# Hybrid mixer and expert trunk on one core: the router fed from raw rows, gain and shift of the norm applied after the first gather

## Chip, cores and metric

One Trainium2 chip, 1 core. The metric is the device time of one execution in microseconds (us), as the median of several runs. PE is TensorE, DVE VectorE, ACT ScalarE, POOL GpSimd, SP SyncE.

## The reference, cut to what matters

Two layers over 256 tokens of width 1024. Each adds a mixer and then a channel mixer to alpha times x, with a layer norm after each. The channel mixer of layer 0 is a dense SwiGLU, that of layer 1 picks two of eight experts for each token.

```python
for l in range(DEPTH):
    mix = hybrid_mixer(x, ...)
    x = layer_norm(DEEPNORM_ALPHA * x + mix, ln1_g[l], ln1_b[l])
    ffn = swiglu(x, ...) if l % 2 == 0 else moe_swiglu(x, router_w[j], router_b[j], ...)
    x = layer_norm(DEEPNORM_ALPHA * x + ffn, ln2_g[l], ln2_b[l])

def layer_norm(x, g, b):
    mu, var = mean(x), mean((x - mean(x)) ** 2)
    return (x - mu) * rsqrt(var + LN_EPS) * g + b

# in moe_swiglu, for each token
logits = xt @ router_w + router_b
top_logit, top_idx = lax.top_k(logits, 2)
top_w = softmax(top_logit)
# each expert: (silu(xb @ wg) * (xb @ wu)) @ wd, weighted and added to the token's row
```

## The kernel before, in words

**Data.** Tokens lie in two tiles t of 128 rows; a row of 1024 is cut into 8 blocks k of 128, or two halves of 512. Weights stream through the core in pieces of 128x2048 (1 MB), 33 for the dense part and for each expert: A and B hold gate and up weights, D the down weights (FFORDER). SP's queue loads them into 17 slots, each as soon as its last user is through. To keep float32 accuracy, ACT copies each half of a piece rounded into whi (high part, ring of 3 pieces) and DVE subtracts to get low. A product is then three matmuls: high by high, high by low, low by high (L639 to L641; L832, L835, L838 for down pieces). This "split" is one ACT and one DVE operation of 128x1024 for each half piece. Activations are split in the same way.

**Expert jobs.** Eight jobs of one expert each, classes W and N in turn. A wide job (W, 128 token slots) splits its weights, a narrow one (N, 64 slots) uses them raw, with matmuls of L981 and L990. Job 0 is wide and always expert 7, so that its weights can be loaded before the router is done. In a wide job each engine runs through the 33 pieces i (L1030 on PE, L1400 on ACT, L1880 on DVE). At step i ACT and DVE split piece i + 2. After pieces B of chunk c, ACT makes silu (L1408), DVE the product he (L1883), PE transposes it (L853), ACT and DVE split the transpose (L1403, L1887), and a D piece uses it. Each engine works strictly in the order written; DVE's he of chunk c stands at step i = 3c + 1 (c over 0), ahead of the splits of that step. In job 0, steps 5 and 8 of ACT also make xh, steps 6 and 9 of DVE xl (L1850), the split rows of x for later gathers; step 22 of DVE makes S for the next job (L1843, L1845), for which it waits for POOL's places (tab_rdy, L1899); after piece 25 PE gathers rows for the next job.

**The second mixer's end and the router.** PE adds the last products of the mixer to PSUM tile by tile (down, L817). DVE's norm (L1544) takes mean and variance from PSUM (L1552, L1556), ACT the root (L1189), DVE the normed rows with gain and shift into x (L1562, L1566). PE transposes x (L623), ACT and DVE copy it to xT (L1197, L1534), PE multiplies by the router's weights (L1103). DVE adds the bias, finds the two largest of eight (L1803 to L1809), makes the one-hot mask mk (L1817). PE counts ranks with a triangular matrix (L1119 to L1121), DVE makes the selection matrix S (L1843), PE gathers and transposes the rows of job 0 in one step, x by S (L939), ACT and DVE split them to xgh and xgl (L1363, L1855), and job 0 begins. All steps take both tiles together. Between them PE runs filler products that nobody reads (keep_warm, L633; their numbers in WARM). DVE then makes the weights and hands counts over to POOL (tables, L1824 to L1834); POOL makes the order of jobs, the places of the tokens and their weights in some 70 small operations (job_tables, L491 to L579). ACT puts alpha times x into acc (L1355) during the router.

## Time and profile before

| what | value |
|---|---|
| median of 3 runs | 1027.97 us (1027.78 to 1028.08) |
| the profiled execution | 1027.9 us, its span 1026.1 us |
| mean granted TensorE clock | 0.996 |
| weights moved | 318 pieces of 1 MB, 334 GB/s over the span |
| last product of the second mixer to first product of job 0 | 352.03 to 366.73 us |
| job 0 on PE | 366.73 to 464.4 us |

The span is from the first to the last instruction; the 1.8 us around it belong to the execution. In the timeline a row merges equal operations; its second number is the time from the first one's start to the last one's end. Matmuls overlap, so the pitch from start to start is shorter than the duration shown.

### The profile page before, as it was taken

To read this page: it belongs to the slowest core of one execution; us is meant where nothing else is said; L and a number is where in the kernel's file an instruction comes from. 1 tells how busy PE (TensorE), PEld (TensorE's weight loads), DVE (VectorE), ACT (ScalarE), POOL (GpSimd) and SP (SyncE) were. 2 spreads that over 40 slices of the span, in tenths; PEclk is the share of its full clock that TensorE was granted. 3 is DMA by queue.
4 is the path that set the end of the run, shared out by engine and by line. 5 is a ranking of instruction groups with operands and counts; after the bars stand their busy time and mean duration, and the time that the engine had idled before them with its cause. 6 is when DMAs were issued, how large, how long until landed. Compare 5 with 4: busy or idle time off the path is not lost.

```text
span 1026.1 us, 15030 instructions
## 1 busy us (share of the span) xinstructions
PE 1005.4 (98%) x5878; PEld 765.8 (75%) x5878; DVE 644.9 (63%) x885; ACT 538.7 (52%) x822; POOL 86.0 (8%) x92
## 2 busy tenths in 40 slices
PE   9999999999999999999999999999999999999995
PEld 7977888888798887886567886558887556888552
DVE  6998554545679889981049993119986117997103
ACT  5786343444459677771147772128775116776112
POOL 0002000000200069910000000000000000000000
PEclk9999999999999999999999999999999999999998
DMA  9945454545584659989999999999999999999993
GB/s 370 383 160 210 174 193 177 201 172 201 219 335 148 232 190 352 370 335 395 421 420 421 421 421 421 419 422 421 420 422 422 419 422 421 419 422 421 420 420 149
DMA packets 48153, 343.23 MB, mean 335 GB/s; under 512 B 5376, under 2 KB 5504, under 8 KB 6864
## 3 DMA queue, kind: packets, MB, share of 16 engines
q1 hardware_dynamic: 46800, 337.14, 82.0%
q0 software_dynamic: 848, 4.51, 1.2%
q8 instruction: 48, 0.79, 0.3%
q10 hardware_dynamic: 432, 0.59, 0.2%
q14 instruction: 25, 0.20, 0.1%
HBM read 341.17 MB, written 1.05 MB: 334 GB/s over the span
## 4 chain that ended last, share of the span: by engine, by line
PE 88%; DVE 7%; ACT 3%; issue 1%; POOL 0%; POOLq 0%; DVEq 0%
PE bank L990 15%; PE bank L639 13%; PE bank L641 13%; PE bank L640 13%; PE bank L981 7%; PE bank L832 7%; PE bank L835 6%; PE bank L838 6%; DVE low L1868 2%; PE bank L853 1%; DVE low L1515 1%; PE bank L1072 1%; PE bank L633 1%; PE bank L623 1%; ACT scr L1281 1%
## 5 line engine op out<-in xcount | busy, mean ns | idle before, releaser
L1868 DVE TENSOR_TENSOR low<-raw,whi 128x1024 fp32r<-128x1024 f32 x246 | 290.6, 1235 | 21.6 <-ACT whi L1385 21.3
L1385 ACT ACTIVATE whi<-raw 128x1024 fp32r<-128x1024 f32 x246 | 242.2, 1051 | 0.3 <-PE bank L641 0.3
L990 PE MATMUL bank<-raw,xg 128*64 128x256 f32 x1312 | 150.1, 380 | 0.0
L1515 DVE TENSOR_TENSOR low<-raw,whi 128x1024 fp32r<-128x1024 f32 x110 | 131.3, 1223 | 25.6 <-ACT whi L1169 24.6
L639 PE MATMUL bank<-whi,xgh 128*128 128x512 f32 x352 | 141.7, 402 | 0.0
L1922 DVE TENSOR_TENSOR he<-he,bank 128x128 f32<-128x128 f32 x44 | 12.7, 289 | 202.5 <-ACT he L1445 202.5
L641 PE MATMUL bank<-whi,xgl 128*128 128x512 f32 x352 | 137.7, 391 | 0.0
L640 PE MATMUL bank<-low,xgh 128*128 128x512 f32 x332 | 129.3, 390 | 0.0
L1169 ACT ACTIVATE whi<-raw 128x1024 fp32r<-128x1024 f32 x114 | 115.8, 1058 | 25.2 <-PE bank L641 17.4
L990 PEld LDWEIGHTS bank<-raw,xg 128*64 128x64 f32 x1312 | 92.1, 137 | 43.2 <-issue 2.4
L639 PE MATMUL bank<-whi,ah 128*128 128x512 f32 (+1 forms) x240 | 92.2, 384 | 3.3 <-DVE al L1527 1.9
L641 PE MATMUL bank<-whi,al 128*128 128x512 f32 (+1 forms) x240 | 90.2, 376 | 0.0
L640 PE MATMUL bank<-low,ah 128*128 128x512 f32 (+1 forms) x240 | 90.0, 375 | 0.0
L981 PE MATMUL bank<-raw,hT 128*64 128x512 f32 x336 | 79.6, 594 | 0.0
L1445 ACT ACTIVATE he<-bank 128x128 f32<-128x128 f32 x44 | 12.2, 278 | 125.0 <-PE bank L990 125.0
L639 PEld LDWEIGHTS bank<-whi,xgh 128*128 128x128 f32 x352 | 66.1, 188 | 15.2 <-DVE low L1868 2.7
L641 PEld LDWEIGHTS bank<-whi,xgl 128*128 128x128 f32 x352 | 66.0, 188 | 14.7
L640 PEld LDWEIGHTS bank<-low,xgh 128*128 128x128 f32 x332 | 62.5, 188 | 11.9
L832 PE MATMUL bank<-whi,hth 128*128 128x512 f32 x224 | 70.2, 394 | 0.3 <-DVE htl L1887 0.3
L838 PE MATMUL bank<-whi,htl 128*128 128x512 f32 x224 | 69.1, 390 | 0.0
L835 PE MATMUL bank<-low,hth 128*128 128x512 f32 x216 | 66.7, 390 | 0.0
L639 PEld LDWEIGHTS bank<-whi,ah 128*128 128x128 f32 x240 | 45.2, 188 | 12.2 <-DVE al L1527 2.4
(310 smaller groups left out, 1376.5 us busy)
## 6 DMA issues: line engine op xcount, KB each, us to landing
raw<-W SPq DMA_DIRECT2D x303, 1024.0 KB, 16.7
spare<-W SPq DMA_DIRECT2D x15, 1024.0 KB, 17.8
scr<-gb_d POOLq DMA_DIRECT2D x3, 1024.0 KB, 5.0
x<-x_d SPq DMA_DIRECT2D x2, 512.0 KB, 5.6
raw<-W SPq DMA_DIRECT2D x2, 512.0 KB, 6.0
scr<-wbd_d POOLq DMA_DIRECT2D x2, 512.0 KB, 9.3
spare<-gb_d SPq DMA_DIRECT2D x1, 1024.0 KB, 14.5
out_d<-acc ACTq DMA_DIRECT2D x2, 256.0 KB, 2.5
```

The costliest lines, as they stand in the source:

```text
L639: nc.tensor.matmul(out, sh, mh, start=first, stop=False, skip_group_check=True)
L640: nc.tensor.matmul(out, sh, ml, start=False, stop=False, skip_group_check=True)
L641: return nc.tensor.matmul(out, sl, mh, start=False, stop=last, skip_group_check=True)
L832: nc.tensor.matmul(bank[:, 2 + 2 * t + n, :], sh, wh[:, n * 512:(n + 1) * 512], start=st, stop=False, skip_group_check=True)
L835: nc.tensor.matmul(bank[:, 2 + 2 * t + n, :], sh, wl[:, n * 512:(n + 1) * 512], start=False, stop=False, skip_group_check=True)
L838: last = nc.tensor.matmul(bank[:, 2 + 2 * t + n, :], sl, wh[:, n * 512:(n + 1) * 512], start=False, stop=en, skip_group_check=True)
L981: last = nc.tensor.matmul(bank[n * NARROW:(n + 1) * NARROW, 2, :], hT[:, c % 2, h * NARROW:(h + 1) * NARROW], w[:, h * D + n * 512:h * D + ...
L990: last = nc.tensor.matmul(bank[n * NARROW:(n + 1) * NARROW, c % 2, 0:FC].rearrange("p (a n) -> p a n", a=2), xg[:, kk, at:at + NARROW], gu ...
L1169: nc.scalar.activation(whi[:, p % SPLIT, h * HW:(h + 1) * HW], piece_slot(place(p)[0])[:, h * HW:(h + 1) * HW], ACT.Copy).then_inc(hi_rdy, 1)
L1385: nc.scalar.activation(whi[:, q % SPLIT, h * HW:(h + 1) * HW], piece_slot(home(J, i)[0])[:, h * HW:(h + 1) * HW], ACT.Copy).then_inc(hi_rd ...
L1515: V.tensor_tensor(low_of(p)[:, h * HW:(h + 1) * HW], piece_slot(place(p)[0])[:, h * HW:(h + 1) * HW], whi[:, p % SPLIT, h * HW:(h + 1) * H ...
L1868: V.tensor_tensor(low_slot(s)[:, h * HW:(h + 1) * HW], piece_slot(s)[:, h * HW:(h + 1) * HW], whi[:, q % SPLIT, h * HW:(h + 1) * HW].bitca ...
```

## The change

- **Router from raw rows.** ACT copies the mixer's raw sums y from PSUM into x, half a tile at a time (copy_y). PE transposes these, between the last products of the mixer (down_last), which are reordered so that half a tile is complete early. DVE multiplies the router's weights by the norm's gain and shift (gs, two operations of 128x64), PE adds their columns up, and DVE puts the norm into the logits: root's reciprocal times product, plus an offset from the mean and the column sums.
- **Rows.** ACT turns the raw rows into centred, scaled ones without gain and shift (centre, four operations of 128x512). The gather of job 0 reads these. Gain and shift, now along partitions, are applied after it: for the first half by DVE in four operations of 128x128, for the second by ACT in four (rows_first). The norm's four products of DVE and its copy to xT are gone. x itself gets gain and shift from DVE in four operations of 128x1024 in job 0, steps 3, 6, 9 and 12 (gain_shift); xh moves to ACT's steps 7 and 13, acc to its steps 16 and 19, xl to DVE's steps 17 and 20.
- **Tiles apart.** Choice, rank, S and gather are done for tile 0 and then for tile 1 (picks, places, gather_first). Small operations that took both tiles are now issued twice.
- **Job 0's start.** The splits of its first three pieces are done before it; its first two pieces are multiplied high parts first (first_products). DVE's tables come after all that; the counts of PE after the first piece. POOL no longer waits for x_rdy ahead of its tables, but still for DVE's.
- **Filler.** Of the router's 19 filler products one is left.
- rtab grows by gain and shift (16 columns); yh moves in SBUF, so that gb stays whole until job 0 has used it.

The diff, cut:

```diff
-XH_AT = {5: 0, 8: 1}
+GAIN_AT = {3: (0, 0), 6: (0, 1), 9: (1, 0), 12: (1, 1)}
+XH_AT = {7: 0, 13: 1}
+ACC0_AT = {16: 0, 19: 1}
...
-WARM = {"start": 8, "x1": 5, "mixer": 0, "dense": 0, "last_mixer": 0, "tile": 4, "tile2": 2, "split": 3, "rank": 7,
-        "slots": 3}
+WARM = {"start": 8, "x1": 5, "mixer": 0, "dense": 0, "slots": 1}
...
+            def down_last(p, act_t, t, ph):
+                order = [(0, 0), (0, 1), (1, 0), (1, 1)] if t or ph == 1 else [(0, 0), (1, 0), (0, 1), (1, 1)]
+                for n, k in order:
...
+                    if t == NT - 1 and ph == 1 and (n, k) in ((0, 1), (1, 0)):
+                        transpose_x(ph + 1, 0, (n,))
+                    elif t == NT - 1 and (n, k) == (0, 1):
+                        logits(0, (0,))
+                        column_sums()
+                    elif t == NT - 1 and (n, k) == (1, 0):
+                        transpose_x(ph + 1, 1, (0,))
...
+            def first_products(i, slot, wlow):
+                for k in range(4):
+                    if k % 2 == 0:
+                        pe.wait_ge(lo_rdy, 2 * (STREAM + i) + k // 2 + 1)
+                    if i == 0:
+                        pe.wait_ge(xg0_rdy, k + 1)
+                    elif k == 0:
+                        pe.wait_ge(xgh_rdy, 1)
...
+                pe.wait_ge(xgl_rdy, i + 1)
...
+            def gather_first(t, b, ks=range(4)):
+                pe.wait_ge(z_rdy, 2 * t + b + 1)
...
+                logits(0, (1,))
+                transpose_x(2 * DEPTH - 1, 1, (1,))
+                logits(1, (0, 1))
+                nc.tensor.matmul(bank[:, 1, 0:NE], ones, mk[:, 0, :], start=True, stop=False, skip_group_check=True)
+                pe.wait_ge(S0_rdy, 1)
+                gather_first(0, 0)
                 pe.wait_ge(mk_rdy, 1)
...
+                gather_first(0, 1)
+                keep_warm(WARM["slots"], 6)
+                pe.wait_ge(S_rdy, 1)
+                gather_first(1, 0)
+                gather_first(1, 1)
...
+                copy_y(0, 0)
+                copy_y(0, 1)
+                hi_half(p, 0)
+                root(0)
+                copy_xT(0, 0)
+                copy_xT(0, 1)
+                hi_half(p, 1)
+                copy_y(1, 0)
+                centre(0, 0)
+                copy_xT(1, 0)
+                copy_y(1, 1)
+                centre(0, 1)
+                root(1)
+                copy_xT(1, 1)
+                centre(1, 0)
+                centre(1, 1)
...
+            def rows_first():
+                for k in range(4):
+                    act.wait_ge(xv0_rdy, k + 1)
+                    nc.scalar.activation(xgh[:, k], first_rows[:, k], ACT.Copy).then_inc(xg0_rdy, 1)
+                act.wait_ge(xg0_ps, 2)
+                for k in range(4):
+                    turned_row(first_rows, 1, k).then_inc(xv_rdy, 1)
+                act.wait_ge(xv_rdy, 4)
+                nc.scalar.activation(xgh[:, 4:KT], first_rows[:, 4:KT], ACT.Copy).then_inc(xgh_rdy, 1)
...
+                    sums(0)
+                    stats(0)
+                    lo_half(STREAM, 0)
+                    dve.wait_ge(var_rdy, NT * ph + 1)
+                    minus_mean(0)
+                    lo_half(STREAM, 1)
+                    sums(1, (0,))
+                    lo_half(STREAM + 1, 0)
...
+                    offsets(0)
+                    sums(1, (1,))
+                    stats(1)
+                    picks(0)
+                    dve.wait_ge(var_rdy, NT * ph + 2)
+                    minus_mean(1)
+                    offsets(1)
+                    places(0)
+                    picks(1)
+                    places(1)
+                    return
...
+            def gain_shift(t, a):
+                if a:
+                    dve.wait_ge(xg_step, t + 1)
+                else:
+                    dve.wait_ge(gb_in, 16 * 3)
+                    dve.wait_ge(xg0_ps, 2)
+                V.tensor_tensor(x[:, t, :], x[:, t, :], gb[:, a, :], ALU.add if a else ALU.mult).then_inc(
+                    x_rdy if a else xg_step, 2 if a else 1)
...
-            one_hot([ps_e[:, t, FIRST:FIRST + 1] for t in range(NT)], WIDE)
-            lo_half(STREAM, 1)
+            lo_half(STREAM + 1, 1)
+            dve.wait_ge(xg0_ps, 1)
+            for k in range(4):
+                V.tensor_scalar(first_rows[:, k, :], bank[:, 4, k * P:(k + 1) * P], gainT[:, k:k + 1], shiftT[:, k:k + 1],
+                                ALU.mult, ALU.add).then_inc(xv0_rdy, 1)
+            dve.wait_ge(xv0_rdy, 4)
+            dve.wait_ge(xg0_rdy, 4)
+            rows_low(0)
+            expert_split(0, 2, 0)
+            dve.wait_ge(xgh_rdy, 1)
+            rows_low(1)
+            expert_split(0, 2, 1)
             tables()
-            rows_wide(0, 0)
-            lo(STREAM + 1)
-            dve.wait_ge(acc0_rdy, NT)
```

## Rows read from the trace of the kernel before

**Rows 1.** The page of the kernel before, section 1.

```profile
PE 1005.4 (98%) x5878; PEld 765.8 (75%) x5878; DVE 644.9 (63%) x885; ACT 538.7 (52%) x822; POOL 86.0 (8%) x92
```

**Rows 2.** Busy time by stretch: stretch, its length, busy us (instructions), clock, DMA share, GB/s.

```profile
352.00:366.70 14.70, 14.70 (x110) 13.12 (x109) 11.77 (x35) 6.16 (x10) 0.52 (x3) 1.00 0.45 181
366.70:399.00 32.30, 31.50 (x141) 24.99 (x139) 30.81 (x32) 27.42 (x34) 29.61 (x35) 1.00 0.85 307
399.00:443.00 44.00, 43.70 (x200) 35.92 (x200) 43.57 (x47) 32.93 (x42) 38.11 (x38) 1.00 0.96 365
...
1005.00:1010.00 5.00, 5.00 (x46) 2.85 (x44) 0.29 (x1) 0.76 (x3) 0.00 (x0) 1.00 0.46 195
```

**Rows 3.** Chain of waits, 352 to 368 us: start, us, what.

```profile
352.03 0.88 PE bank L623 x8
...
353.84 1.68 PE bank L1103 x16
...
359.66 1.74 PE bank L633 x7
...
363.30 3.69 PE bank L939 x32
```

**Rows 4.** Timeline, 338 to 368 us: start, us (of all xcount), engine, line, tiles.

```profile
343.58 0.70 PE L832 MATMUL bank<-whi,ah 128*128 128x512 f32 x2
...
345.97 0.61 PE L838 MATMUL bank<-whi,al 128*128 128x512 f32 x2
...
352.07 1.30 DVE L1552 BATCH_NORM_STATS2 bnst<-bank 128x6 f32<-128x512 f32 x2 [0.94 <-PE bank L838]
...
352.51 1.09 ACT L1197 ACTIVATE xT<-bank 128x512 f32<-128x512 f32 x2 [2.10 <-PE bank L623]
...
359.70 0.17 DVE L1803 TENSOR_TENSOR msc<-bank,rtab 128x16 f32<-128x16 f32 x1 [0.55 <-PE bank L1103]
...
361.09 0.17 DVE L1817 TENSOR_TENSOR msc<-msc 128x16 f32<-128x16 f32 x1
...
365.60 0.23 DVE L1834 SCALAR_TENSOR_TENSOR msc<-msc 128x8 f32<-128x8 f32 x1
...
366.73 0.48 PE L639 MATMUL bank<-whi,xgh 128*128 128x512 f32 x1
```

**Rows 5.** Timeline of DVE, 366 to 470 us.

```profile
370.53 3.48 DVE L1868 TENSOR_TENSOR low<-raw,whi 128x1024 fp32r<-128x1024 f32 x3
...
386.42 1.23 DVE L1850 TENSOR_TENSOR xl<-x,xh 128x1024 fp32r<-128x1024 f32 x1
...
431.76 0.41 DVE L1883 TENSOR_TENSOR he<-he,bank 128x256 f32<-128x256 f32 x1
...
435.51 5.48 DVE L1868 TENSOR_TENSOR low<-raw,whi 128x1024 fp32r<-128x1024 f32 x4
440.92 0.41 DVE L1883 TENSOR_TENSOR he<-he,bank 128x256 f32<-128x256 f32 x1
```

**Rows 6.** Timeline of PE at the eighth and ninth transpose of h.

```profile
433.39 0.38 PE L853 MATMUL bank<-ident,he 128*128 128x128 f32 x2
...
441.83 0.38 PE L853 MATMUL bank<-ident,he 128*128 128x128 f32 x2
```

**Rows 7.** Timeline of POOL; busy time by stretch of POOL (two rows), of DVE (last row).

```profile
429.64 1.12 POOL L575 TENSOR_TENSOR msc<-msc,tabs 128x34 f32<-128x34 f32 x1
...
366.00:368.40 2.40, 1.84 (x7) 1.00 0.00 0
368.40:430.80 62.40, 57.82 (x59) 1.00 0.93 343
...
368.40:430.70 62.30, 61.32 (x62) 1.00 0.92 342
```

**Rows 8.** Busy time by stretch at the end of the kernel, columns as in rows 2.

```profile
1016.00:1018.00 2.00, 0.00 (x0) 0.00 (x0) 1.70 (x5) 1.50 (x3) 0.00 (x0) 0.93 0.06 12
1018.00:1020.00 2.00, 0.00 (x0) 0.00 (x0) 1.91 (x5) 1.96 (x4) 0.00 (x0) 0.50 0.00 0
```

More of the change, by code:

```diff
@@ L321, in build @@
         x_rdy = sem("x_rdy")
+        xg_step = sem("x_times_gain")
         xT_ps = sem("xT_ps")
@@ L928, in dense @@
                 pe.wait_ge(hTl0_rdy, 1)
-                down(p + 1, part(NCH - 1), False, True, 0)
+                down_last(p + 1, part(NCH - 1), 0, 1)
                 half(p, 0, NCH - 2, 1)
@@ new lines, in logits @@
+            def logits(t, groups):
+                for g in groups:
+                    pe.wait_ge(xTa_rdy, 2 * t + g + 1)
+                    for k in range(4 * g, 4 * g + 4):
+                        last = nc.tensor.matmul(bank[:, 3 - t, (3 + t) * NE:(4 + t) * NE], xT[:, k, t * P:(t + 1) * P],
+                                                gs[:, 0, k, :], start=k == 0, stop=k == KT - 1, skip_group_check=True)
+                        if t and k == 5:
+                            pe.wait_ge(mk0_rdy, 1)
+                            nc.tensor.matmul(bank[:, 3, 0:NE], tri, mk[:, 0, :], start=True, stop=True,
+                                             skip_group_check=True).then_inc(pos0_ps, 1)
+                if groups[-1] == 1:
+                    last.then_inc(lg_ps, 1)
@@ L1037, in wide_job @@
                     wl = low_slot(home(J, i)[0])
+                    if first and i < 2:
+                        first_products(i, slot, wl)
+                        if i == 0:
+                            counts()
+                        continue
                     for h in range(2):
@@ L1129, in _ @@
             router()
-            pe.wait_ge(S_rdy, 1)
-            for b in range(2):
-                gather_first(b)
             for J in range(NJ):
@@ L1421, in wide_job @@
                         high_x(XH_AT[i])
+                    if first and i in ACC0_AT:
+                        start_of_sums(ACC0_AT[i])
                     if J in EVENT and i == (FIRST_XR_AT if first else XR_AT):
@@ L1426, in wide_job @@
                     for h in range(2):
-                        if i + 2 < FFP:
+                        if i + 2 < FFP and not (first and i == 0):
                             expert_split(J, n, i + 2, h)
```

280 lines of the change are left out of this document (175 added, 105 removed).

## The prediction

> **What bounds the kernel now.** I read the page's busy times first, then the busy times by stretch, then the chain of waits and the timeline of each engine. PE is busy 98% of the span [rows 1], so only PE's idle, its filler and its late starts can be saved. Between the last product of the second mixer (352.03 us) and the first product of the first expert job (366.73) PE is busy without a gap [rows 2], but the chain shows with what: 8 transposes, 16 logits products, filler products of L633 (seven in one row, 19 in all), 32 small gathers [rows 3]. These 14.7 us are the router, and all the change can attack. They end in a DVE sequence: logits at 359.70, choices at 361.26, counts and weights at 365.83 [rows 4].
>
> What follows matters as much. In 366.70 to 399 DVE is busy 30.81 of 32.30 us, in 399 to 443 43.57 of 44.00 [rows 2]; PE shows 0.8 us of idle in the first and next to none later. DVE splits two half pieces per piece of weights, and PE's transposes of h wait behind them for DVE's product he. At PE's eighth transpose (433.39) that product was done at 431.76 + 0.41 = 432.17, a slack of 1.2 us; at the ninth (441.83) it was done at 441.33, a slack of 0.5 [rows 5, 6]. So job 0 runs on PE with DVE 0.5 to 1.2 us behind it: whatever the router gives, DVE must follow, and the change puts more work on DVE just there.
>
> The weights' DMA is not the bound at the end: in 1005 to 1010 its share is down to 0.46 [rows 2], so the last piece lands near 1007 and PE uses it about 3 us later. A shift of job 0 moves frees and requests together.
>
> **The head, step by step.** Times are in the trace of before.
> *Tail of the mixer.* The last products run at (345.97 - 343.58)/10 = 0.24 us from start to start, a small wait included [rows 4]. Put among them: 12 transposes at 0.11 (0.88 for eight), 4 logits and one column sum at 0.105 to 0.115 (1.68 for 16, 3.69 for 32) [rows 3]. With 0.1 for waits the mixer's end moves from 352.03 to about 354.0; that is paid back, since this work followed it before.
> *ACT.* Four raw copies, 0.6 each (the price of xT's copies, 1.09 for two [rows 4]), and four centrings of the same size. Tile 0's lie beside products, tile 1's centrings beside DVE's choice. The last raw copy needs the last product (354.0) and ends at 354.6.
> *DVE.* Tile 1's statistics: 0.65 + 0.2, to 355.75 with the waits. Gone from there are four norm products (2.8) and copy_x. Choice of tile 0: six linked small operations; eleven took 359.70 to 361.26 for both tiles [rows 4], so 1.3, to 357.05. Minus mean, offset 0.6; place and S of tile 0 0.65; choice of tile 1 1.3, to 359.6; its place 0.9, to 360.5. The weight difference 0.17 and a half split 1.15: 361.8. Four scaled gathers of 128 columns have no row; between 0.15 (a small operation) and 0.7 (a 512 column one) I take 0.22, as S of the same size has 0.24: 362.75. Low part 0.69 after ACT's high copies, split, low part, split: 366.75. Tables, moved behind all this, 1.82 as before (364.01 to 365.83): **368.6**, 2.8 later than 365.83.
> *PE.* The gathers of tile 0 are over before S of tile 1 exists; the last ends at 361.5. First product 362.45 instead of 366.73; two pieces of 12 products each at 0.23 to 0.24 put the third piece of before at 372.4, and now, with two short waits, at 368.2: **4.2 us earlier**. The removed filler costs nothing unless the clock falls (below).
>
> **Job 0 on DVE.** From the first split of piece 2 (370.53) to the eighth he (431.76) took 61.23 us: 44 half splits, two xl, 14 small ones and about 1 us of waits [rows 5]. After the change DVE enters at 368.6; the two splits of piece 2 are done (-2.35), four gain and shift operations of 128x1024 are added. They have no row; the nearest is xl, same size, two SBUF operands, 1.23 long and 1.15 from start to start [rows 5]: +4.6. With other operands they could hardly be under 0.7 (a 512 one) or over 1.5 (a split beside POOL's large operations takes 1.35 [rows 5]): +2.8 to +6. Sum: 368.6 + 61.2 - 2.35 + 4.6 = 432.0, less the waits, most of which go when DVE lags: 431.2. So DVE reaches this point **no earlier than before (431.76), and PE's slack of 1.2 is all that is left of 4.2**: the eighth transpose at about 432.1, 1.3 earlier. acc and xh only change places on ACT, which is busy 32.93 of 44 [rows 2]: nothing, while DVE is behind it.
>
> *POOL's tables.* Next, at piece 22, DVE makes S of the following job and waits for POOL's places. POOL had them at 429.64 + 1.12 = 430.76, 1.3 before DVE asked [rows 5, 7]. After the change it starts at 368.7. In the trace POOL did 7 operations in 2.4 us, at 0.26 each, where DVE was idle for half of it, then some 58 more in 62.4 us at 0.98 each, beside 62 of DVE's [rows 7]: next to a busy DVE it gets one operation done for one of DVE's. DVE will now be busy from the first. It runs 63 before it asks (42 half splits, 4 gains, 2 xl, 15 small), POOL needs 65: some 3 operations remain, which take 0.25 to 0.5 each with DVE at rest, so DVE waits 1 to 1.5 us. The order of the jobs, also POOL's, is wanted by SP's queue only when piece 16 of job 0 is freed, in the middle of the job: nothing. POOL's old wait for x before the tables goes, but it waited for DVE's weights anyway (365.83). From there to the ninth he is 440.92 - 431.76 = 9.16 us: 431.2 + 9.2 + 1.2 + 0.4 = 442.0, against PE's 441.83 before. After it DVE has room again: no gain operation is left, and POOL's tables end.
>
> Of 4.2 us at the start, about 0 remains: I put -0.1 to +0.4, say **+0.2**. The profiled execution took 1027.9 (span 1026.1 and 1.8 around it), 0.07 under the median 1027.97. Forecast 1028.1.
>
> **The rule I weigh.** The rows show POOL going from 0.26 to 0.98 us per operation beside DVE's splits, and DVE's splits from 1.14 (three in 3.48) to 1.35 from start to start (four in 5.48) beside POOL's large ones [rows 5, 7]. The Trainium skill, SBUF, State Buffer, section "SBUF: two separate sides", says the port pair of VectorE and GpSimd is an exclusive lock held for a whole instruction, taken by VectorE operations with two SBUF inputs too. By it each added gain operation locks POOL out as well, so the tables can only get later; the sum would then end in the case of late tables below, 1029.5 or more, instead of 1028.1. The trace agrees as far as it goes; it speaks against the change.
>
> **Rivals.**
> *1. DVE keeps up (faster).* POOL has its places in time, or its operations collide less with DVE's splits. Of the 61.23 us above, 2.3 are the two xl, 4.6 the 14 small ones at 0.33, 1 the waits, so a split took 1.21 on average, against 1.14 undisturbed [rows 5]. Without the wait the ninth transpose comes 1.1 earlier (1027.0); with no collisions at all, 42 x 0.07 = 2.9 us more: 1024, where PE's own lead of 4.2 ends it. For it: DVE will come to piece 22 a little behind ACT and free of its waits. Against: POOL's work is the same. Midpoint 1025.6, chance 0.27; over 0.2% faster only if most collisions go.
> *2. Late tables (slower).* Place: DVE's wait for places at piece 22. If POOL needs a full turn for every operation, it is 7 x 1.15 - 2.4 = 5.6 later, on top of 2.8: 439; DVE's rest from 431.7 on shortens what is left (7 operations) to 3 us: places at 434.8, three us of wait, job 0 ends 1.8 later. It decides from 433.0 on; every further us is a us. 1029.5 to 1030.5, chance 0.16.
> *3. The clock falls (slower).* Between 355.4 and 362.4 PE now has some 35 short instructions and one filler product. In the trace the granted clock fell from 1.00 to 0.50 (1.2 GHz) in 1016 to 1018, with PE at rest [rows 8]. If it falls, the 24 products of the first two pieces take up to twice 0.23: at most 5.5 us, PE's third piece at up to 373 and no lead left; with the DVE work behind it the end comes 2 to 3.5 later: 1030.7. Against it: no single gap will be over about 1.3 us. Chance 0.12. The Trainium skill, TensorE: Matmul & The Clock Gate, section "Why this matters for your kernels", asks only that long idle gaps be kept out; by it the clock would hold.
> *4. The edit does less than it says.* If the two tiles' steps queue up behind each other, DVE's head is 1 to 2 us longer and all of it shows, for DVE is the bound: 1029.5. The opposite, the whole 4.2 kept (1023.7), needs an idle DVE, which the rows exclude.
>
> **The numbers.** Forecast case 0.40 (1027.3 to 1029.2), rival 1 0.27, rival 2 0.16, rival 3 0.12, rival 4 0.05. One measurement tells 0.2%, 2.05 us, from nothing. Faster by that is most of rival 1: 0.22. Slower: half of rival 2, nearly all of rival 3, some of 4 and of the forecast's own spread: 0.27. Same: 0.51. The range leaves out the cases beyond 1025.2 and 1030.8, one in ten each. The unknown costs (gain operations -1.8 to +1.4, scaled gathers -0.3 to +2) are in it.
>
> **What the profile would show.** Right: first product of job 0 near 362.5 and tables' last operation near 368.6; PE idle before transposes of h through piece 22, released by DVE; a DVE wait for POOL near 431 to 433; ninth transpose within 1 us of 441.8; from there every later stage shifted by the same amount. Wrong: DVE idle before piece 20 (the lead then survives), a clock under 1.00 between 358 and 368, or a DMA wait in the narrow jobs.

## The result, and the profile after

The changed kernel takes **1032.26 us** (median of 6 runs, 1031.51 to 1032.91) against 1027.91 for the kernel before on the same chip: ratio 1.0042, 95% interval 1.0029 to 1.0054. It is slower by 4.35 us. The forecast was 1028.1 with a range up to 1030.8, so the time lies outside. The profiled execution took 1031.51 us (span 1029.7), the lowest of the six.

**A gain ahead of the router.** By 338 us the changed kernel is 1.03 us ahead: POOL's load of gb for the router starts at 336.86 for 337.89. This is a part of the change that neither my list of it nor my sum has. down_last is used at the end of the dense part too and puts PE's transposes of tile 0 between the last products there, so that PE no longer waits before the second mixer (first line before, second line after):

```profile
276.50 0.50 PE L639 MATMUL bank<-whi,ah 128*128 128x512 f32 x1 [0.97 <-DVE al L1527]
275.19 0.39 PE L662 MATMUL bank<-whi,ah 128*128 128x512 f32 x1
```

No run has this part alone, but it is no chance of one profile: POOL's load starts at 336.61 to 336.96 in all eleven runs below that are built on after, and at 337.89 to 338.08 in before and the four built on it. So a time of after below compares with one of before, or with one of my forecast, only when 1.03 us is added to it, and from 338 us on the change loses about 1.03 us more than the medians show.

The page, sections 1 and 4, first of after:

```profile
PE 1004.0 (98%) x5862; PEld 763.6 (74%) x5862; DVE 646.9 (63%) x898; ACT 545.8 (53%) x838; POOL 85.7 (8%) x92
...
PE 82%; DVE 7%; POOL 6%; ACT 3%; issue 1%; DMA 1%; POOLq 0%; SPq 0%; DVEq 0%; ACTq 0%
```

and the same line of section 4 (the chain that ended last, by engine) of before:

```profile
PE 88%; DVE 7%; ACT 3%; issue 1%; POOL 0%; POOLq 0%; DVEq 0%
```

The busy times hardly differ from [rows 1]. The chain does: 6% of the span, some 62 us, now runs through POOL, about the length of POOL's tables. What was off the path in before has come onto it.

**The head.** Busy time by stretch of after; columns as in [rows 2], the number before the DMA share is the granted clock:

```profile
355.00:358.00 3.00, 2.48 (x21) 2.30 (x21) 2.59 (x17) 2.18 (x4) 0.00 (x0) 1.00 0.93 388
358.00:361.00 3.00, 3.00 (x18) 2.82 (x17) 2.27 (x10) 2.64 (x5) 0.00 (x0) 0.57 0.67 284
361.00:364.00 3.00, 2.95 (x20) 2.66 (x20) 1.43 (x5) 0.74 (x3) 0.00 (x0) 0.86 0.00 0
364.00:367.00 3.00, 3.00 (x17) 2.56 (x16) 2.40 (x4) 2.96 (x8) 0.00 (x0) 1.00 0.01 3
```

and its timeline there (start, us of all xcount):

```profile
357.60 1.34 PE L1007 MATMUL bank<-S,x 128*128 128x128 f32 x8
...
359.28 2.05 PE L1007 MATMUL bank<-S,x 128*128 128x128 f32 x8
...
359.74 0.29 DVE L1778 TENSOR_SCALAR S<-rtab,msc 128x128 fp32r<-128x128 f32 x1
...
360.99 0.77 PE L656 MATMUL bank<-ah 128*128 128x512 f32 x1
361.56 2.09 PE L1007 MATMUL bank<-S,x 128*128 128x128 f32 x16
362.80 1.37 DVE L2136 TENSOR_SCALAR xr<-bank,rtab 128x128 f32<-128x128 f32 x4 [1.57 <-PE bank L1007]
...
363.69 0.47 PE L907 MATMUL bank<-whi,xgh 128*128 128x512 f32 x1
```

DVE's choice is nearly as fast as worked out: S of tile 1 stands at 360.0, on the clock of before 361.1, where I had 360.5. But PE is not ready for it. The granted clock falls from 1.00 to 0.50 (from 2.4 to 1.2 GHz) at 358.4 and is back at 361.9. Eight gathers take 2.05 us after 1.34 for the eight before them, and those of tile 1 begin only at 361.56. DVE stands 1.57 us waiting for them, and the first product of job 0 comes at 363.69, on the clock of before 364.7, not 362.45.

**Job 0.** DVE of after, and POOL's first and last operation ahead of DVE's S:

```profile
368.69 0.16 DVE L2002 COPY msc<-bank 128x8 f32<-128x8 f32 x1
...
370.28 0.23 DVE L2009 SCALAR_TENSOR_TENSOR msc<-msc 128x8 f32<-128x8 f32 x1
...
371.56 0.42 DVE L2072 TENSOR_TENSOR he<-he,bank 128x256 f32<-128x256 f32 x1
...
375.74 1.21 DVE L2044 TENSOR_TENSOR x<-x,scr 128x1024 f32<-128x1024 f32 x1
...
432.71 0.41 DVE L2072 TENSOR_TENSOR he<-he,bank 128x256 f32<-128x256 f32 x1
436.35 0.37 DVE L2018 TENSOR_SCALAR S<-rtab,msc 128x64 fp32r<-128x64 f32 x1 [3.23 <-POOL msc L596]
...
445.28 0.41 DVE L2072 TENSOR_TENSOR he<-he,bank 128x256 f32<-128x256 f32 x1
```

```profile
370.61 1.14 POOL L538 TENSOR_SCALAR tabs<-msc 128x8 f32<-128x8 f32 x1 [33.21 <-DVE msc L2009]
...
435.99 0.26 POOL L596 TENSOR_TENSOR msc<-msc,tabs 128x34 f32<-128x34 f32 x1
```

PE's eighth and ninth transposes of h (for before see [rows 6]), and two of the waits on PE and DVE in 366 to 440 us (total, times, longest):

```profile
433.17 0.44 PE L921 MATMUL bank<-ident,he 128*128 128x128 f32 x2 [0.86 <-DVE he L2072]
...
445.74 0.44 PE L921 MATMUL bank<-ident,he 128*128 128x128 f32 x2 [1.11 <-DVE he L2072]
```

```profile
PEld bank L921 <- DVE he L2072: 4.9, 6, 1.3
DVE S L2018 <- POOL msc L596: 3.2, 1, 3.2
```

Against [rows 5]: he is 2.4 us earlier in its first use (371.56 for 373.94; 1.03 of this is the gain ahead of the router), 0.95 later in its eighth (432.71 for 431.76), and 4.4 later in its ninth (445.28 for 440.92). So DVE lost 3.3 us on the way through job 0, and then 3.4 more at one place, the wait for POOL. The narrow job starts at 468.48 instead of 464.44, 4.0 later (5.1 lost since 338 us); at the end of the profiled execution 3.6 of it is left.

### The profile page after: what moved, and what is told of

It is laid out like the page before. It is cut to its first block, busy times and chain, and to the rows that moved or that the text cites. A ratio compares the mean times of both kernels' runs of the same rounds, so it can differ in the third digit from the quotient of the medians.

```text
span 1029.7 us, 15039 instructions
## 1 busy us (share of the span) xinstructions
PE 1004.0 (98%) x5862; PEld 763.6 (74%) x5862; DVE 646.9 (63%) x898; ACT 545.8 (53%) x838; POOL 85.7 (8%) x92
## 4 chain that ended last, share of the span: by engine, by line
PE 82%; DVE 7%; POOL 6%; ACT 3%; issue 1%; DMA 1%; POOLq 0%; SPq 0%; DVEq 0%; ACTq 0%
PE bank L1083 15%; PE bank L662 12%; PE bank L664 12%; PE bank L663 11%; PE bank L1074 7%; PE bank L880 6%; PE bank L886 6%; PE bank L883 6%; PE bank L921 1%; DVE low L1653 1%; PE bank L1170 1%; DVE low L2057 1%; POOL tabs L534 1%; POOL tabs L535 1%; PE bank L646 1%
## 5 line engine op out<-in xcount | busy, mean ns | idle before, releaser
L662 PE MATMUL bank<-whi,xgh 128*128 128x512 f32 x344 | 138.4, 402 | 2.2 <-DVE low L2057 2.2
L664 PE MATMUL bank<-whi,xgl 128*128 128x512 f32 x344 | 134.5, 391 | 0.0
L663 PE MATMUL bank<-low,xgh 128*128 128x512 f32 x324 | 126.3, 390 | 0.0
L1578 ACT ACTIVATE hT<-bank 128x128 f32<-128x128 f32 x44 | 12.2, 277 | 80.0 <-PE bank L1170 80.0
```

What stands on the lines that cost most here:

```text
L662: nc.tensor.matmul(out, sh, mh, start=first, stop=False, skip_group_check=True)
L663: nc.tensor.matmul(out, sh, ml, start=False, stop=False, skip_group_check=True)
L664: return nc.tensor.matmul(out, sl, mh, start=False, stop=last, skip_group_check=True)
```

## The experiments

In the expectations T is my theory as it stood at that time and R its rivals. All kernels are compared with the kernel before on the same chip (1027.98 to 1028.04). The last column is the start and length in us of the stretch in which the granted clock was 0.50 in the profiled execution, read from stretches of 1 us. In the runs with the fillers of before there is none. Where it is there, its length differs between kernels with the same code ahead of it, and with it the time of the first product of job 0: 363.69 with 3.4 us at half clock (after), 364.84 and 364.70 with 6.8 us (e3, e10); 365.47 with 6.8 us (e1), 366.37 and 366.32 with 10.2 us (e5, e8). So one profile's times in the head are set beside another's only where this stretch is alike.

| run | built on | median us | ratio (95%) | narrow job starts | half clock |
|---|---|---|---|---|---|
| before | | 1028.0 | 1 | 464.44 | none |
| after | | 1032.26 | 1.0042 (1.0029 to 1.0054) | 468.48 | 358.4, 3.4 |
| e1 tables early | after | 1029.95 | 1.0018 (1.0009 to 1.0028) | 467.09 | 357.4, 6.8 |
| e3 selection at step 24 | after | 1029.90 | 1.0017 (1.0007 to 1.0027) | 467.30 | 356.2, 6.8 |
| e8 = e1 and e3 | after | 1029.77 | 1.0017 (1.0007 to 1.0026) | 467.12 | 356.6, 10.2 |
| e12 tables between | after | 1031.62 | 1.0037 (1.0023 to 1.0052) | 468.51 | 357.7, 6.8 |
| e4 tables late | before | 1031.48 | 1.0034 (1.0021 to 1.0046) | 467.95 | none |
| e9 four more operations | before | 1032.20 | 1.0041 (1.0027 to 1.0056) | 468.91 | none |
| e5 = e1, no gain and shift | after | 1027.54 | 0.9997 (0.9987 to 1.0006) | 465.02 | 356.7, 10.2 |
| e10 no gain and shift | after | 1029.71 | 1.0014 (1.0005 to 1.0023) | 466.49 | 356.4, 6.8 |
| e7 no filler | before | 1033.36 | 1.0051 (1.0033 to 1.0069) | 469.99 | 356.3, 13.7 |
| e2 11 fillers | after | 1033.04 | 1.0049 (1.0032 to 1.0066) | 469.88 | 357.8, 3.4 |
| e6 = e1, 17 fillers | after | 1029.63 | 1.0019 (1.0009 to 1.0029) | 466.64 | none |
| e11 = e6, no gain and shift | after | 1027.96 | 1.0002 (0.9993 to 1.0011) | 466.28 | 358.1, 3.4 |
| e13b xl late | before | 1028.34 | 1.0004 (0.9995 to 1.0013) | 464.85 | none |
| e14b = e1, acc and xl late | after | 1028.72 | 1.0005 (0.9996 to 1.0014) | 465.98 | 356.2, 10.2 |
| e15b = e14b, half the gain late | after | 1030.00 | 1.0028 (1.0013 to 1.0043) | 466.25 | 358.7, 6.8 |

### The place of the tables

**e1**: DVE's tables ahead of the gathered rows, the counts on PE ahead of tile 0's second gather.

```diff
             lo_half(STREAM + 1, 1)
+            tables()
             dve.wait_ge(xg0_ps, 1)
...
             expert_split(0, 2, 1)
-            tables()
```

> The changed kernel with one thing moved: the counts of PE right after tile 1's rank, and DVE's tables right after the first half split of piece 1, in the time in which DVE waits for the gathers, so that POOL starts about 7 us earlier. Theory T (late tables: DVE's 3.2 us wait for POOL's places at step 22 of job 0 sets the loss): POOL starts near 363 instead of 370.6, the wait at step 22 is gone, job 0 ends 2.5 to 3.5 us earlier, time near 1029. Rival D (the four added gain and shift operations fill DVE, and the wait only stands where DVE's own lag would show anyway): under 1 us gained, time 1031 to 1032. Rival C (the clock's fall between 358 and 364 us makes the loss): nothing gained, 1032.

Measured: 1029.95, 2.3 us less than after. Its DVE beside its POOL (the timeline):

```profile
363.41 0.26 POOL L538 TENSOR_SCALAR tabs<-msc 128x8 f32<-128x8 f32 x1 [26.16 <-DVE msc L2008]
...
364.57 1.36 DVE L2136 TENSOR_SCALAR xr<-bank,rtab 128x128 f32<-128x128 f32 x4 [1.25 <-PE bank L1007]
...
426.10 0.26 POOL L596 TENSOR_TENSOR msc<-msc,tabs 128x34 f32<-128x34 f32 x1
...
435.45 0.41 DVE L2071 TENSOR_TENSOR he<-he,bank 128x256 f32<-128x256 f32 x1
435.78 0.24 DVE L2017 TENSOR_SCALAR S<-rtab,msc 128x64 fp32r<-128x64 f32 x1
```

POOL has the places at 426.4, over nine us before they are wanted, and the wait is gone, as T said; the time is 0.95 over T's 1029. In exchange DVE comes later to step 22. The first he is at 373.04 instead of 371.56, but 1.1 of this is the longer half clock: e3, with the same 6.8 us of it and late tables, has 372.71. The eighth he (435.45) is 1.6 behind that of e3 (433.87). Why DVE needs 1.3 us more on that way the runs don't show.

**e3, e8**: the selection of the next job moved behind the wait instead; e8 has both edits.

```diff
-FIRST_S_AT = 22
-FIRST_XR_AT = 26
-FIRST_GATHER_AFTER = {25: 0, 28: 1}
+FIRST_S_AT = 24
+FIRST_XR_AT = 29
+FIRST_GATHER_AFTER = {28: 0, 30: 1}
```

> The changed kernel with the selection matrix of the next job made at step 24 of job 0 instead of 22, and the gather behind it after pieces 28 and 30 instead of 25 and 28; tables stay late. DVE asks POOL about 5.5 us later. Theory T: the wait of 3.2 us goes, though POOL's tables are as late as before; 2 to 3.5 us gained, 1028.8 to 1030.3. Rival D: the lag is DVE's own work, nothing gained, 1032. A small loss of its own is possible if the gather, now nearer to the end of job 0, is late for job 1.

> Tables early and the selection matrix at step 24. If POOL is in time at step 22 already with early tables (theory T, as the first experiment's missing wait says), this changes nothing more: 1029.5 to 1030.3. If some wait for POOL was still hidden in the collisions: up to 1 us faster.

e3 gives 1029.90 with a wait of 0.9 for POOL instead of 3.2, e8 1029.77. Two ways to take the same wait away give the same time, and both together no more: the late tables are worth 2.3 us, and the other 2 lie elsewhere.

**e12**: tables between the gathered rows' first subtraction and the splits of the third piece.

```diff
             rows_low(0)
+            tables()
             expert_split(0, 2, 0)
...
             expert_split(0, 2, 1)
-            tables()
```

> The changed kernel with the tables after the first subtraction of the gathered rows and ahead of the third piece's splits, and the counts after tile 1's ranks: GpSimd can begin about 2 us before the 370.6 of the changed kernel, without delaying the gathered rows as the early tables did. T: GpSimd starts at 368 to 369, the wait at step 22 is 0 to 1.2 us, first product at 363.5 to 365, the third piece 1 to 2 us later than in the changed kernel; 1029.3 us (1028.6 to 1030.3), since VectorE is then the bound as with the early tables, and a place of the tables can't help beyond that. Rival R1: the 1 us earlier first product comes through to the end: 1028.2 to 1028.6, level with the kernel before. Rival R2: the later third piece costs as much as the wait saved: 1031 to 1032.

1031.62: a miss of T, with R2's time but not its reason. POOL starts at 368.91, 2.8 earlier than in e3, which has the same length of half clock, and the first he (372.94) is only 0.2 later than there. But DVE still waits 2.0 for the places: what is gained is 1.2 us of wait and no more. The runs agree: at mean clocks of 0.993 to 0.994 this kernel takes 1031.29 to 1031.62, and after 1032.66 to 1032.91. Starting at 368.91, POOL has DVE's splits beside it at once. In e1 the tables stand where DVE would wait for PE anyway, and POOL's first nine operations take 0.20 to 0.38 us each.

**e4**: the late tables alone, on the kernel before.

```diff
-            tables()
             rows_wide(0, 0)
             lo(STREAM + 1)
+            tables()
```

> The kernel before with one part of the change alone: DVE's tables after the first rows' low part and the splits of piece 1, about 6 us later. Theory T: POOL loses its 7 fast operations and starts near 372, DVE waits 3 to 6 us at step 22, time 1030.5 to 1033, although DVE has no gain operations and PE its fillers. Rivals C and D: no more than 0.5 us slower than 1027.9, as nothing of their causes is in it.

1031.48, a loss of 3.4 us, inside T's range, but by another split than T's: the wait was to be 3 to 6 us. POOL starts at 372.63, DVE enters job 0 1.85 later (first he 375.79), is 2.5 later at the eighth he (434.22), and then waits only 1.2:

```profile
435.79 0.38 DVE L1843 TENSOR_SCALAR S<-rtab,msc 128x64 fp32r<-128x64 f32 x1 [1.16 <-POOL msc L575]
```

### Gain and shift on DVE

**e9**: four operations of the same size added to DVE's part of job 0 in the kernel before.

```diff
+                    if first and i in (3, 6, 9, 12):
+                        t = i // 3 % 2
+                        V.tensor_tensor(acc[:, t, :], acc[:, t, :], acc[:, t, :], ALU.max)
```

> The kernel before, with four operations of 128x1024 added to VectorE's part of job 0, at steps 3, 6, 9 and 12 (each the larger of acc and acc, which changes nothing): the four gain and shift operations alone, without anything else of the change. My theory T now says that VectorE's 4.7 us of added work cost about 2.4 us of end, since VectorE has about half of that to spare between job 0's transposes: 1030.4 us (1029.5 to 1031.2), the late transposes of h 1.5 to 3 us behind those of before, the last before the narrow job at 466 to 467 instead of 464.4. Rival R1: the kernel before has more slack (its head is not crowded), and the addition is absorbed: 1028.0 to 1028.4. Rival R2: the whole 4.7 us show: 1032.5.

1032.20, a loss of 4.2 us: a miss of T (1030.4) and near R2. Nothing else of the change is in it, the clock stays at 1.00, and DVE has no wait for POOL. The stretches 373.5 to 402 and 402 to 433, columns as in [rows 2], of before:

```profile
373.50:402.00 28.50, 27.41 (x124) 21.73 (x123) 27.95 (x31) 23.70 (x31) 26.22 (x30) 1.00 0.96 355
402.00:433.00 31.00, 31.00 (x141) 25.51 (x140) 30.57 (x34) 23.80 (x30) 28.84 (x29) 1.00 0.95 358
```

and of e9, with one of the four and the wait on PE that they make:

```profile
373.50:402.00 28.50, 25.06 (x110) 19.44 (x109) 28.02 (x29) 21.59 (x27) 26.21 (x30) 1.00 0.87 323
402.00:433.00 31.00, 29.39 (x133) 23.81 (x134) 31.00 (x31) 22.78 (x30) 28.99 (x27) 1.00 0.89 339
```

```profile
387.50 1.31 DVE L1904 TENSOR_TENSOR acc<-acc 128x1024 f32<-128x1024 f32 x1
```

```profile
PEld bank L853 <- DVE he L1883: 6.9, 6, 2.2
```

DVE was busy for 58.5 of 59.5 us before the addition. It can't take more; PE does 14 and 8 products less in the same stretches, and the eighth transpose comes at 437.87 instead of 433.39, 4.5 later for about 4 x 1.2 = 4.8 us of added work.

**e5, e10**: gain and shift applied to 8 of 1024 columns, with the tables early (e5) and where the change has them (e10). In both, gain and shift are left out for the other 1016 columns of x after the second mixer's norm; all else is computed.

```diff
-                V.tensor_tensor(x[:, t, :], x[:, t, :], gb[:, a, :], ALU.add if a else ALU.mult).then_inc(
+                V.tensor_tensor(x[:, t, 0:8], x[:, t, 0:8], gb[:, a, 0:8], ALU.add if a else ALU.mult).then_inc(
```

> Tables early as in the first experiment, and the four gain and shift operations on 8 of 1024 columns only: gain and shift of x are left out on the other columns. Theory D2 (with the tables early, DVE's added 4.6 us in job 0 set the rest of the loss, 1.9 us): DVE is no longer late for PE's transposes after step 8, 2.5 to 4.5 us gained on 1029.95, so 1025.5 to 1027.5, under the kernel before. Rival C2 (the rest of the loss is the clock and the late first product alone): under 1 us gained.

> The changed kernel with gain and shift applied to 8 of 1024 columns (left out elsewhere, so job rows after job 0 and the residual are not normed fully), tables left where the change has them. T says that the wait for GpSimd's tables at step 22 then takes what VectorE saves: VectorE arrives 2 to 4 us earlier at step 22 but the tables come no earlier, so that the wait grows from 3.2 to about 6 us and the time is 1031 to 1032, within 1.2 us of the changed kernel. Rival R1, that the tables run at the pace of VectorE's operations, so that fewer and shorter ones on VectorE let them end earlier too, and the two costs simply add up: 1029.6 to 1030.2, with a wait of 3 to 4 us.

e5: 1027.54, 2.4 below e1. e10: 1029.71, 2.55 below after, with this at step 22:

```profile
431.71 0.41 DVE L2072 TENSOR_TENSOR he<-he,bank 128x256 f32<-128x256 f32 x1
434.40 0.38 DVE L2018 TENSOR_SCALAR S<-rtab,msc 128x64 fp32r<-128x64 f32 x1 [2.29 <-POOL msc L596]
```

T was wrong here, R1 right in its mechanism and its time (its wait of 3 to 4 us is 2.3). POOL starts 1.0 later than in after (371.60), by the longer half clock, and yet has the places 1.95 earlier. Against e3, whose head and half clock are the same, DVE is 2.2 us earlier at step 22 (eighth he 431.71 for 433.87). POOL's pace hangs on DVE's work, so the two costs hardly hide each other: 2.3 + 2.5 = 4.8, and removing both (e5) takes 4.7 off. By medians, that is: e10 at mean clocks of 0.992 to 0.994 (1029.63 to 1029.91) is 3.0 below after at 0.993 to 0.994.

### The clock

**e7**: the kernel before without filler. **e2**: after with 11 fillers from 355.5 us. **e6**: e1 with 17 fillers, five of them around tile 1's second transposes, three ahead of tile 0's S. **e11**: e6 with gain and shift left out as in e5.

```diff
-WARM = {"start": 8, "x1": 5, "mixer": 0, "dense": 0, "last_mixer": 0, "tile": 4, "tile2": 2, "split": 3, "rank": 7,
-        "slots": 3}
+WARM = {"start": 8, "x1": 5, "mixer": 0, "dense": 0, "last_mixer": 0, "tile": 0, "tile2": 0, "split": 0, "rank": 0,
+        "slots": 0}
```

e2:

```diff
+                        if t and k == 3:
+                            keep_warm(2, 6)
...
+                keep_warm(2, 6)
                 pe.wait_ge(S0_rdy, 1)
                 gather_first(0, 0)
+                keep_warm(3, 6)
...
-                keep_warm(WARM["slots"], 6)
+                keep_warm(4, 6)
```

e6 and e11:

```diff
+                keep_warm(1, 0)
                 transpose_x(2 * DEPTH - 1, 1, (1,))
+                keep_warm(4, 0)
                 logits(1, (0, 1))
...
+                keep_warm(3, 0)
                 pe.wait_ge(S0_rdy, 1)
                 gather_first(0, 0)
+                keep_warm(4, 0)
...
-                keep_warm(WARM["slots"], 6)
+                keep_warm(5, 0)
```

> The kernel before without its 19 fillers in the router, nothing else. Theory C: the clock falls there too, 32 gathers (3.7 us) and the first products take up to twice as long, 2.5 to 5 us lost: 1030.5 to 1033. Rival: DVE's own work in job 0 takes the delay in, or the clock holds: within 1 us of 1028.0.

> The changed kernel with 11 filler products instead of 1 in the router, put where PE waits (2 in tile 1's logits, 2 ahead of S of tile 0, 3 behind the first gather, 4 ahead of S of tile 1). Theory C (clock): granted clock stays at 1.00 through 358 to 364, tile 1's gathers take 1 us less, and the whole kernel gains what the fall cost, 3 to 4 us: 1028.5. Theory T: the first product of job 0 comes about 1 us earlier, POOL starts 1 us earlier, and the time falls by that 1 us and no more: 1030.8 to 1031.3; the spread over runs (1031.5 to 1032.9) shrinks.

> Tables early, and 17 fillers instead of 1, the first of them 1 and 4 around tile 1's second transposes (354 to 356), then 3, 4 and 5. The earlier set of 11 began at 355.6 and the clock fell all the same at 358. Theory C3 (what PE does before 356 decides the fall): granted clock 1.00 throughout, gathers of tile 1 in 1.85 us instead of 2.65, first product about 1.5 us earlier, time 1028.0 to 1029.0 and a narrow spread. If DVE's work alone sets the end: time unchanged at 1030 within 0.5, clock 1.00. If fillers push the choice steps: up to 1 us lost.

> The changed kernel with early tables, 17 fillers in the router and gain and shift on 8 of 1024 columns only (left out elsewhere): the whole head of the change, at a clock that does not fall, without VectorE's addition. T: 2.3 us below the one with fillers and full gain and shift, 1027.3 us (1026.6 to 1027.8), narrow job from 464.2 to 464.8: the first product is 1.4 us earlier than in the kernel before, and hardly any of it reaches the end. Rival R1: the lead at the first product comes through once gain and shift are gone: 1025.6 to 1026.6, narrow job from 463.0.

Granted clock, in the rows of e7, e2, e6 and e11, in this order:

```profile
355.00:358.00 3.00, 2.21 (x13) 1.86 (x12) 1.72 (x4) 0.75 (x2) 0.00 (x0) 0.71 0.96 404
358.00:361.00 3.00, 3.00 (x16) 3.00 (x15) 1.82 (x2) 1.33 (x2) 0.00 (x0) 0.50 0.31 131
```

```profile
355.00:358.00 3.00, 3.00 (x22) 2.69 (x22) 2.59 (x17) 2.12 (x4) 0.00 (x0) 0.96 0.93 377
358.00:361.00 3.00, 3.00 (x12) 2.71 (x12) 0.90 (x6) 2.61 (x4) 0.00 (x0) 0.50 0.70 295
```

```profile
355.00:358.00 3.00, 3.00 (x26) 2.82 (x24) 2.19 (x14) 2.05 (x4) 0.00 (x0) 1.00 0.90 366
358.00:361.00 3.00, 3.00 (x21) 2.68 (x21) 1.34 (x9) 2.68 (x4) 0.00 (x0) 1.00 0.70 298
```

```profile
358.00:361.00 3.00, 3.00 (x12) 2.72 (x12) 1.10 (x7) 2.42 (x3) 0.00 (x0) 0.52 0.61 259
```

The filler of before is worth 5.4 us to it (e7: the first product at 371.15 instead of 366.73, with 13.7 us at half clock).

In the changed kernel fillers that begin at 355.5 come too late: the clock falls in the same place, for the same 3.4 us as in after, and the fillers in it run at 1.2 GHz. They only stand in PE's way. The first product is at 365.17, 1.5 later than in after, and 1033.04 is worse than after: a miss of both T and C.

Those of e6, which begin at 354.2, hold the clock at 1.00 in its profile, and give 0.3 us against e1, inside the spread. Its first product is at 365.36; e1's, with 6.8 us at half clock, at 365.47, those of e5 and e8, with 10.2, at 366.37 and 366.32. So the fillers take most of the time that the clock would have given back.

e11 is not the clean test that it was meant to be. Its profiled execution took 1029.38, and in it the clock fell for 3.4 us in spite of the 17 fillers. Its eleven runs stand in two groups: eight at 1027.72 to 1028.09 with mean clocks of 0.996 to 0.997, three at 1029.31 to 1029.41 with 0.995. The median, 1027.96, is just above T's range (1026.6 to 1027.8).

Such groups tell what the clock is worth within one kernel. After has three runs at 1031.51 to 1031.86 with a mean clock of 0.996, and three at 1032.66 to 1032.91 with 0.993 to 0.994. e3 has five at 1029.08 to 1029.41 with 0.995, and five at 1030.40 to 1030.62 with 0.993 to 0.994. A lower mean clock, as a longer fall gives it, goes with 1.1 to 1.4 us more at the end; that it is the fall in the router in the runs without a profile too is likely, not shown. What no fall at all would give to after is not shown, for each way to hold the clock that was tried put fillers before the first product.

### Where a lead goes in job 0

**e13b**: xh and xl behind the full stretch, in the kernel before. **e14b**: e1 with acc and xl there. **e15b**: also gain and shift of tile 1.

```diff
-XH_AT = {5: 0, 8: 1}
+XH_AT = {23: 0, 26: 1}
```

```diff
-ACC0_AT = {16: 0, 19: 1}
+ACC0_AT = {22: 0, 25: 1}
```

```diff
+GAIN_AT = {3: (0, 0), 6: (0, 1), 21: (1, 0), 23: (1, 1)}
+XH_AT = {7: 0, 24: 1}
+ACC0_AT = {24: 0, 26: 1}
```

and in all three:

```diff
+FIRST_XR_AT = 29
+FIRST_GATHER_AFTER = {28: 0, 30: 1}
```

> The kernel before with the two splits of x (ScalarE's xh and VectorE's xl) moved from steps 5/6 and 8/9 of job 0 to steps 23/24 and 26/27, the gather of the next job's rows after pieces 28 and 30 instead of 25 and 28. Theory T now: every operation of VectorE ahead of step 22 of job 0 moves the end by nearly its own length, in either direction, since VectorE is busy for 98% of that stretch; after step 22 it has slack. T: the eighth he and transpose of h come 1.2 to 2 us earlier (432.1 at the latest instead of 433.39), and the time is 1026.2 to 1027.0. Rival R1: PE's own pace of 8.44 us for each chunk bounds that stretch too, and the operation is only a shift of waiting: 1027.6 to 1028.1. Rival R2: the later gather holds up the narrow job: over 1028.3.

> The changed kernel with early tables, and with acc and xl moved from steps 16/19 and 17/20 of job 0 to 22/25 and 23/26, the gather after pieces 28 and 30. T: 1.5 to 2.4 us below early tables alone (1029.95), so 1027.5 to 1028.5, level with the kernel before, with 3.6 us of PE's waits for he shrinking to under 2. Rival R1: no gain, 1029.5 to 1030.2, if what binds there is the lock with GpSimd's tables or ScalarE.

> As the run before, and gain and shift of tile 1 moved from steps 9 and 12 to steps 21 and 23, with acc at 24 and 26, xl at 25 and 27: VectorE's added work spread over both sides of step 22. T: 1026.5 to 1027.6, faster than both kernels, as one more operation of 1.15 us leaves the full stretch. Rival R1: the work after step 22 no longer fits (3.5 us of xl and gain in two chunks with about 1 us of slack each), and the last transposes of h and the gather come later: 1027.8 to 1029.

PE of e13b at the eighth and ninth transposes and the narrow job's first product:

```profile
432.28 0.38 PE L853 MATMUL bank<-ident,he 128*128 128x128 f32 x2
441.65 0.44 PE L853 MATMUL bank<-ident,he 128*128 128x128 f32 x2 [0.78 <-DVE he L1883]
...
464.85 1.95 PE L990 MATMUL bank<-spare,xg 128*64 128x256 f32 x16
```

The eighth transpose is 1.1 us earlier for 2.4 us taken away: from the third transpose on (389.92, 398.36, 406.98, 415.42, 423.85, 432.28) PE runs at its own pace, 8.4 to 8.6 us for a chunk, as R1 had it. Then the same work costs what it had saved: the narrow job starts 0.4 later than in before, and the time, 1028.34, is at R2's limit of 1028.3 and a miss of T (1026.2 to 1027.0). Extra work shows at nearly full price (e9), work taken away gains only until PE's own pace binds, and behind step 22 there is less room than I took from the stretches.

e14b gains 1.2 over e1, 0.2 past the upper end of what T allowed, and is level with the kernel before. e15b, 1030.00, shows R1's mechanism and is 1.0 past R1's range: its eighth transpose is early (431.65), and the ninth comes 10.6 us later. No version beats the kernel before: e5, e11, e13b and e14b can't be told from it, and two of these leave work out. Those built on after even have the gain of about 1.1 us at the dense part's end in them. The kernel before with that gain alone was not run; by the 1.03 us it should take about 1026.9, an estimate.

In e5 one can follow where the lead goes. DVE of e5:

```profile
417.58 1.21 DVE L2025 TENSOR_TENSOR xl<-x,xh 128x1024 fp32r<-128x1024 f32 x1
...
423.77 0.41 DVE L2071 TENSOR_TENSOR he<-he,bank 128x256 f32<-128x256 f32 x1
...
426.76 1.21 DVE L2025 TENSOR_TENSOR xl<-x,xh 128x1024 fp32r<-128x1024 f32 x1
...
433.47 0.41 DVE L2071 TENSOR_TENSOR he<-he,bank 128x256 f32<-128x256 f32 x1
```

Its sixth transpose, at 414.59, is 1.9 us ahead of before (1.1 of this from the dense part's end). Then come the two chunks into which the change has put xl, and they take 9.65 and 9.70 us from transpose to transpose instead of PE's 8.44: at the eighth (433.94) it is 0.55 behind.

## Why the prediction was wrong

Two steps failed: the rate of POOL's operations beside DVE's, and with it DVE's wait at step 22 (3.2 us for 1.2), and the head of PE, where short products at half clock stood in the sum at full speed (the tables' end 2.9 us late). The forecast's times stand on the clock of before. Those of after are given here with 1.03 us added, for the gain ahead of the router.

**The head of DVE and PE: failed.** "The last ends at 361.5. First product 362.45" and "Tables ... 368.6". S of tile 1 was 0.6 late, but the gathers of tile 1 started 1.5 us after S, because PE's queue still held the slowed gathers of tile 0 and the one filler. The first product (364.7) was 2.3 late, the third piece (370.75 for 368.2) 2.6, the tables' end (371.5 for 368.6) 2.9. The mis-sized term is PE's small work at half clock, which stood in my sum at full speed.

**The clock: given 0.12, and it happened.** The trace does not show a gap for it: PE's longest wait in 352 to 370 was 0.4 us. The Trainium skill, TensorE: Matmul & The Clock Gate, section "Why this matters for your kernels", asks for no long idle gaps; by that rule the clock should have held here. It fell to 0.50 at 358.4, so by this measurement the rule is not the only thing to heed. That the fall alone sets the end, as rival 3 had it, is not borne out: e1 and e3 gain 2.3 us and e5 4.7 with longer falls in their profiles than after. But it has a share. The three runs of after with the lower mean clock take 1.1 us more, and the median lies between the two groups.

**Job 0 on DVE: right.** From the tables' end to the eighth he I had 431.2 - 368.6 = 62.6 us; measured 432.71 - 370.51 = 62.2. The gain operations took 1.21 to 1.44 us each, against 1.15 from start to start. That the four of them would be paid for by the lead, and that no slack stood behind it, was right, and e9 shows the price without a lead: 4.2 us. Since entry and wait were wrong, the +0.2 of the sum had nothing to stand on.

**POOL's tables: the step that failed most.** "Next to a busy DVE it gets one operation done for one of DVE's" and "some 3 operations remain ... DVE waits 1 to 1.5 us." DVE waited 3.2. POOL in after (times as in its profile), beside busy DVE and beside waiting DVE:

```profile
370.60:433.20 62.60, 58.01 (x58) 1.00 0.92 350
433.20:436.40 3.20, 2.65 (x8) 1.00 0.94 384
```

DVE ran the 63 operations that I had counted, but POOL got only 58 of its 65 done beside them, and 7 were left (the eighth in the row comes after the places). The pace was there to be read: [rows 7] show POOL's operations of 62.4 us beside 62 of DVE's as 59, and that rate gives 60 for 63. I had rounded it up to one for one. Rival 2 named this place and a wait of three us, with the places at 434.8 (measured 437.3), but with DVE already in time before it.

The experiments bear the mechanism out: without the wait the kernel is 2.3 us faster (e1, e3). On the pace the trace agrees with the Trainium skill, SBUF, State Buffer, section "SBUF: two separate sides" (an exclusive lock for a whole instruction): small operations of POOL take mostly 1.0 to 1.2 us beside DVE and 0.22 to 0.3 with DVE at rest. By that rule I had priced 1029.5 or more, and the measured time is on its side.

**The dense part's end: a term left out.** It gave 1.03 us, in the kernel's favour.

**The sum.** Ninth he forecast at 442.0 - 0.4 = 441.6, measured 446.3, 4.7 late: 2.5 up to the eighth he, from the head, and 2.2 behind it, 2.0 of them from the longer wait. The forecast of +0.2, this 4.7 and the 1.03 gained make 3.9; the profiled execution is 3.6 slower than that of before, and the median 4.35, with a lower mean clock in half of the runs. In a ledger by medians: late tables cost 2.3 (e1, e3), gain and shift 2.4 to 2.5 (e5, e10), and the rest of the change, clock and dense part's end included, gives back about 0.4 (e5 against before, 0.46 between medians, inside the interval). As the dense part's end alone gives about 1.1, by these numbers the new router's head gains nothing by the end of the kernel. On the kernel before the same two cost 3.4 (e4) and 4.2 (e9), 7.6 if they add, which was not run. What remains open is what after would take with a clock that never falls, and how its loss divides between the clock and the rest in the runs that have no profile.

## What to carry to other kernels

Before work is moved off a path, look at who is busy beside the next stretch: an engine at 98% there takes any lead as its own, and prices each added operation at nearly its full length. When a hand-over to a slow helper is put later, count its turns beside the busy engine at the rate that the trace shows, not its time alone, and put the hand-over where that engine waits anyway (e1). Filler that looks like waste may hold the clock (e7: 5.4 us); but filler ahead of the first product takes most of what the held clock gives (e6), and begun too late it gives nothing (e2). Compare the granted clock of two profiles before their times. And find a point ahead of the change where both profiles should agree: where they don't, the change reaches further than its list says.

## What the runs showed of the hardware that I had not expected

- The granted clock fell to 0.50 with PE shown busy for 2.48 of 3.00 us before and without a wait over 0.4 us, amid short products of 8 and 128 columns (after, 355 to 361); fillers starting at 355.5 did not stop it (e2), and the same 17 fillers from 354.2 held it in one profile (e6) and not in another (e11).
- With the same code ahead of it the fall lasted 3.4 us in one profile (after) and 6.8 in others (e3, e10), and the runs of one kernel stand in two groups 1.1 to 1.4 us apart, the slower with the lower mean clock (after, e3, e11).
- POOL's pace follows DVE's instructions so closely that it had the places after 62.7 us instead of 65.6 when four of DVE's long operations had become short (e10: 371.60 to 434.30; after: 370.61 to 436.25), and after 69.1 when DVE did not wait at step 22 (e3: 371.75 to 440.81).
- Removals were nearly additive (medians: 2.3 and 2.5 give 4.7), additions to a full engine nearly full price (4.2 for 4.8).
